# First layer: lower halves of the weights, keys, squares and mix halves move from GpSimd and VectorE

## The chip, the cores and the metric
The kernel runs on one core of one Trainium2 chip. The metric is device time in microseconds of one execution; a comparison uses medians of several. TensorE (PE) multiplies, VectorE (DVE) and ScalarE (ACT) work elementwise, GpSimd (POOL) works elementwise and issues DMAs, SyncE (SP) issues DMAs.

## The reference, cut to what matters
Two transformer-like blocks run one after the other. The change lies in the first layer of the first block, on 512 tokens and 256 tokens of context (768 columns):

```python
def even_mixer(hl, hc, w_in, lb, onorm_w, vnorm_w, ws, bs, w_out, with_ctx):
    pl = hl @ w_in                      # q, v, two z, g, u, v2
    ...
def hgrn2_features(p, lb):
    f = jnp.maximum(lb[d] + (1.0 - lb[d]) * jax.nn.sigmoid(z), F_MIN)
    log_f = jnp.log(f)
    k = 1.0 - f                         # the keys
# gla_chunked: per chunk, cumulated log_f, decays exp(b), scores, state update
def hgrn2_readout(o, g, onorm_w):
    o = rms_norm(o.transpose(0, 2, 1, 3), onorm_w).reshape(bsz, t_len, A_WIDTH)
    return (o * jax.nn.silu(g.astype(jnp.float32))).astype(g.dtype)
def chunk_mlp(u_pre, v_pre, vnorm_w, ws, bs):
    u = jax.nn.gelu(u_pre)
    v = rms_norm(jax.nn.gelu(v_pre)..., vnorm_w)
    sv = jnp.einsum('gts,bnsgc->bntgc', ws, v) + bs.T[:, :, None]
```

## The kernel before
Every operand of a large product is split into an upper half (rounded by ScalarE, `w_hi`) and a lower half (what is left, raw minus upper, `w_lo`); three matmuls make the product. `Flow` (from line 213) streams weight tiles of 128x1024: SyncE loads `w_raw` into two buffers, ScalarE makes `w_hi` at L337, VectorE makes `w_lo` at L393 or, where `low_on_pool` is set, GpSimd at L378, and TensorE multiplies (L456 in this stage). SyncE loads the next tile into a buffer once both halves of the old one are made. A flow has eight turns for each tile; an event is put at a turn, and `weave` merges several generators into one program for each engine by a list of nominal times. Each engine works its program off in order. Upper halves come at turn 1 (`split_turn`), one tile ahead of the products that use them.

`recurrence_and_mix` is the stage from 198 to 449 us. It weaves four things: the flow `uv` (8 tiles, gelu at L1450 by ScalarE), the flow `evg` (4 tiles, silu at L1583), the gated recurrence `Recurrence` (12 steps n over six chunks of 128 in two directions) and `ChunkMix` (4 groups). There are 13 lower halves in the stage: one at the start, one for each of the 12 tiles (two ahead).

A step n of the recurrence is spread over slots of 14.3 nominal us with eight turns. VectorE: `keys` (L1197, turn 3, three slots ahead), `sums` (scans, L1206, turn 7), `base_and_ends` (L1227, L1232), `levels` (L1216, L1217), `decayed_base` (L1244, L1245), `decayed` (L1255 to L1258), `merge` (L1277, L1280), `both` (L1288) and `update` of the state (L1298). ScalarE: `log` (L1310), `grow_base` and `grow` (L1318 to L1327), `keys_back` (L1332). TensorE: `read_out` (L1357, L1358), `gain` (L1365), transposes of the keys (L1374, waits for the update before), `scores` (L1385), `base_scores` (L1405). `keys(n)` waits for `mixed`, which `decayed(n-2)` gives, as both use the same buffer.

`ChunkMix`: ScalarE squares (L1474) and takes roots (L1480, L1485); VectorE norms (L1547); TensorE sums squares (L1510), transposes (L1524) and mixes (L1535); the gate product is L1460. `keep_busy` (L57) issues unread matmuls as fillers.

`GatedReadout` is the next stage, to 472.5 us. For four heads: squares of the output (L1640 by VectorE for heads 0 and 1, L1659 by GpSimd for 2 and 3), sums on TensorE (L1698), roots by ScalarE (L1680, L1683), norm (L1647) and gate product (L1653) by VectorE, upper half by ScalarE (L1673), lower half by VectorE (L1644). The four halves of the mix: upper by ScalarE (L1669), lower by GpSimd (L1662). TensorE ends with fillers once the last roots are made. The stage ends when all engines have ended. Then `eo` multiplies by `ev_out` (L474).

Of the kernel before, what the change touches and what calls it, by code (L numbers as in the profile page):

```python
# [4 lines left out]
F32 = mybir.dt.float32  # L5
F32R = mybir.dt.float32r
ALU = mybir.AluOpType
# [5 lines left out]
DT = D // P  # L13
# [201 lines left out]
class Flow:  # L215
# [10 lines left out]
    def __init__(self, K, c, name, w, n, kt, rhs_hi, rhs_lo, t0, T, on_act, on_dve, nxt, extra="", side=None,  # L226
                 rms_of=None, acc=None, after=None, split_turn=1, parts=1, then=1, ready=None, scaled=None,
                 makes=None, square=None, rms_ps=None, low_on_pool=False):
        nc = K.nc
# [5 lines left out]
        self.on_act, self.on_dve, self.split_turn, self.ready = on_act, on_dve, split_turn, ready  # L235
        self.given_acc, self.scaled, self.makes, self.low_on_pool = acc, scaled, makes, low_on_pool
        if acc is not None and acc[0].shape[1] == 1024:
            first = 512 - Scaled.PAIR - CTX
            self.acc = [a[:, first:first + Scaled.PAIR + T] if scaled is not None else a[:, 1024 - T:1024]
                        for a in acc]  # L240
        else:
            self.acc = [a[:, 0:T] if parts == 1 else a[:, :] for a in acc] if acc is not None else [
                c.enter_context(nc.psum_tensor(f"{name}_acc{j}", [P, 1024], F32))[:, 1024 - T:1024] for j in range(2)]
# [139 lines left out]
    def dve(self, dve):  # L383
# [30 lines left out]
        events = [(turn, lambda i, f=f: f(dve, self, i)) for turn, f in self.on_dve]  # L414
        events.append((self.split_turn, lambda i: split(i + 2)))
        if self.makes is not None:
# [685 lines left out]
class Recurrence:  # L1102
# [82 lines left out]
    def dve(self, dve):  # L1185
# [7 lines left out]

        def keys(n):
            if n >= 2:
                dve.wait_ge(self.mixed, n - 1)
            nc.vector.tensor_scalar(self.heads(self.k[n % 2]), self.of_z(n), -1.0, 1.0,  # L1197
                                    ALU.mult, ALU.add).then_inc(self.k_done, 1)

        def sums(n):  # L1200
# [90 lines left out]
        def update(n):  # L1291
# [4 lines left out]
            for h in range(H):  # L1296
# [4 lines left out]
            last.then_inc(self.updated, 1)  # L1301
        yield from self.turns({0: [(0, merge)], 1: [(1, decayed_base)], 2: [(1, decayed)], 3: [(3, keys)],
                               4: [(0, both), (0, update)], 5: [(2, base_and_ends)], 6: [(2, levels)], 7: [(3, sums)]})

    def act(self, act):
        nc, NL = self.nc, self.NL

        def log(n):
            act.wait_ge(self.k_done, n + 1)
            nc.scalar.activation(self.of_z(n), self.of_z(n), ACT.Ln).then_inc(self.logged, 1)  # L1310
# [242 lines left out]
def recurrence_and_mix(K, A, h_hi, h_lo, q, v, z, y_mlp, weights, x, g, nxt):  # L1553

    nc = K.nc
    with ExitStack() as c:
# [6 lines left out]
        def taken(name, n, work):  # L1563
# [9 lines left out]
                    [(1, cm.gelus)], [(2, cm.gate)],  # L1573
                    (A["ev_g"], DT), acc=acc, parts=2, low_on_pool=True)
        space = [(cm.mixed, 2 * B_GROUPS), (cm.normed, B_GROUPS), (cm.gated, B_GROUPS - 1), (cm.gated, B_GROUPS)]

        def gates(act, f, i):
            act.wait_ge(*space[i])
            for part in range(2):
# [5 lines left out]
        flow_g = Flow(K, c, "evg", A["ev_g"], A_HEADS, DT, h_hi, h_lo, 0, TOK, [(1, gates)], [], nxt, acc=acc, parts=2,  # L1585
                      after=flow, then=2, low_on_pool=True)
        tile = 196 / (2 * B_GROUPS + A_HEADS + 1)
# [8 lines left out]
        with K.block() as block:  # L1596
            @block.sync
            def _(sp):
                gl.sp(sp)
                cm.sp(sp)  # L1600
                weave([], flow.sp(sp))
                weave([], flow_g.sp(sp))

            @block.gpsimd
            def _(pool):
                flow.pool(pool)
                flow_g.pool(pool)

            @block.scalar
            def _(act):  # L1610
                weave(order, flow.act(act), flow_g.act(act), gl.act(act), cm.act(act, flow))

            @block.vector
            def _(dve):
                weave(order, flow.dve(dve), flow_g.dve(dve), gl.dve(dve), cm.dve(dve))

            @block.tensor
            def _(pe):
                weave(order, flow.pe(pe), flow_g.pe(pe), gl.pe(pe), cm.pe(pe))


class GatedReadout:


    def __init__(self, K, c, o, g, weights, y_mlp, hi, lo):
        nc = self.nc = K.nc
        self.K, self.o, self.g, self.weights, self.y_mlp, self.hi, self.lo = K, o, g, weights, y_mlp, hi, lo
        self.sq = c.enter_context(nc.sbuf_tensor("gr_sq", [P, A_HEADS, TOK], F32))
        self.roots = c.enter_context(nc.sbuf_tensor("gr_roots", [P, 2, TOK], F32))
        self.ps = [c.enter_context(nc.psum_tensor(f"gr_ps{j}", [P, 1024], F32)) for j in range(A_HEADS)]  # L1630
        (self.squared, self.squared_late, self.total, self.logged, self.rooted, self.normed, self.gated, self.hi_done,
         self.mlp_hi) = K.signals(
             "gr", "squared squared_late total logged rooted normed gated hi_done mlp_hi")

    SQUARED = 2

    def dve(self, dve):
        nc, H, o = self.nc, A_HEADS, self.o
        for h in range(self.SQUARED):
            nc.vector.tensor_tensor(self.sq[:, h, :], o[:, h, :], o[:, h, :], ALU.mult).then_inc(self.squared, 1)  # L1640

        def lower(h):
            dve.wait_ge(self.hi_done, h + 1)
            nc.vector.tensor_tensor(self.lo[h], o[:, h, :], self.hi[h].bitcast(F32), ALU.subtract)  # L1644
        for h in range(H):
            dve.wait_ge(self.rooted, h + 1)
            nc.vector.scalar_tensor_tensor(out=o[:, h, :], in0=o[:, h, :], scalar=self.weights[:, h:h + 1],  # L1647
                                           in1=self.roots[:, h % 2, :], op0=ALU.mult,
                                           op1=ALU.mult).then_inc(self.normed, 1)
            if h:  # L1650
                lower(h - 1)
            dve.wait_ge(self.normed, h + 1)
            nc.vector.tensor_tensor(o[:, h, :], o[:, h, :], self.g[h], ALU.mult).then_inc(self.gated, 1)  # L1653
        lower(H - 1)

    def pool(self, pool):
        nc, H, o = self.nc, A_HEADS, self.o
        for h in range(self.SQUARED, H):
            nc.gpsimd.tensor_tensor(self.sq[:, h, :], o[:, h, :], o[:, h, :], ALU.mult).then_inc(self.squared_late, 1)  # L1659
        for h in range(H):  # L1660
            pool.wait_ge(self.mlp_hi, h + 1)
            nc.gpsimd.tensor_tensor(self.lo[H + h], self.y_mlp[:, h, :], self.hi[H + h].bitcast(F32), ALU.subtract)  # L1662

# [26 lines left out]
    def pe(self, pe):  # L1690
        nc, H = self.nc, A_HEADS
        for h in range(H):
            if h < self.SQUARED:
                pe.wait_ge(self.squared, h + 1)
            else:
                pe.wait_ge(self.squared_late, h + 1 - self.SQUARED)
            for col, width in ((256, 256), (512, 512)):
# [7 lines left out]
def layer0(K, nc, A, x, x_back, col, cols, mods, mod0, scale1, y_hi, y_lo):  # L1705
# [6 lines left out]
    with ExitStack() as even_:  # L1712
# [4 lines left out]
        with ExitStack() as hctx:  # L1717
# [22 lines left out]
            with ExitStack() as c:  # L1740
                r = GatedReadout(K, c, q, g, col("onorm"), y_mlp, [y_hi[:, m, :] for m in range(DT)],
                                 [y_lo[:, m, :] for m in range(DT)])
                with K.block() as block:  # L1743
                    @block.sync
                    def _(sp):
                        sp.dma_start(x[:, 0:4, :], A["x"][:, 0:4, :]).then_inc(x_back, 16)
                        for h, k in enumerate(tiles):
                            sp.wait_ge(r.gated, h + 1)
                            sp.dma_start(x[:, k, :], A["x"][:, k, :]).then_inc(x_back, 16)

                    @block.gpsimd
                    def _(pool):
                        r.pool(pool)

# [2175 lines left out]
```

## Time and profile before
| | us |
|---|---|
| timed, median of 3 runs | 2685.71 (2684.73 to 2686.37) |
| the profiled execution | 2684.99 |
| its span | 2682.8 |
| mean granted clock of TensorE | 0.986 |
| PE, DVE, ACT, POOL busy | 2529.6, 1682.8, 988.9, 159.0 |

The rows of a timeline are: start in us, duration in us, engine, line, operation, output and inputs by the program's names, shapes, how many were merged into the row, and in brackets the idle time of the engine before it with what ended it. A row of the windows is: from:to, its length, busy us and count of PE, PEld (weight loads), DVE, ACT, POOL, then the granted clock of TensorE, the DMA share and GB/s. A row of the waits is: engine and what waited, who released it, us in total, times, longest. A row of the groups of instructions is: count, busy us, mean ns | idle time before and who ended it.

### The profile page before, as it was taken

The numbers are of one execution on the slowest core, as the hardware profiler recorded it, in microseconds if no ns is written. First come the engines' busy times: TensorE is split into PE (matmuls) and PEld (weight loads), VectorE is DVE, ScalarE is ACT, GpSimd is POOL, SyncE is SP. The second block draws the span as 40 slices with busy tenths as digits, with TensorE's granted clock in tenths as the row PEclk, the third lists the DMA queues.
The fourth block names the chain that finished last, engine by engine and source line by source line (L and its number), as shares of the span: only waits on it lengthen the run. The fifth ranks groups of instructions, "written<-read, shape, count | busy, mean of one in ns | idle before, by whom it ended". The sixth has DMA issues, their size and how long they took to land. (4 is left out here: it accounts for less than half of the span.)

```text
span 2682.8 us, 36507 instructions
## 1 busy us (share of the span) xinstructions
PE 2529.6 (94%) x14797; PEld 2135.6 (80%) x14797; DVE 1682.8 (63%) x2710; ACT 988.9 (37%) x1362; POOL 159.0 (6%) x167
## 2 busy tenths in 40 slices
PE   7999998999999999988999999999989988989997
PEld 2888887888888888865679989977778886867786
DVE  4887697467777776544446756746977774354744
ACT  4225565332212222344344322325542224344532
POOL 0110112000000000000000000000600000000000
PEclk9999999999999999999999999999999999999998
DMA  6650011323343333221013444322220000212232
GB/s 241 191 164 32 25 32 48 103 87 91 104 146 125 103 98 107 75 68 50 1 55 117 130 148 126 124 81 79 79 73 9 17 17 32 102 52 70 80 104 82
DMA packets 62680, 232.25 MB, mean 87 GB/s; under 512 B 6961, under 2 KB 9649, under 8 KB 61874
## 3 DMA queue, kind: packets, MB, share of 16 engines
q1 hardware_dynamic: 47538, 175.40, 20.1%
q0 software_dynamic: 14976, 54.53, 6.6%
q8 instruction: 117, 1.92, 0.3%
q14 instruction: 49, 0.40, 0.1%
HBM read 227.02 MB, written 2.10 MB: 85 GB/s over the span
## 5 line engine op out<-in xcount | busy, mean ns | idle before, releaser
L393 DVE TENSOR_TENSOR w_lo<-w_raw,w_hi 128x1024 fp32r<-128x1024 f32 (+4 forms) x271 | 334.5, 1234 | 375.0 <-ACT w_hi L337 370.8
L337 ACT ACTIVATE w_hi<-w_raw 128x1024 fp32r<-128x1024 f32 (+4 forms) x284 | 298.1, 1050 | 258.8 <-PE late_acc L474 93.4
L474 PE MATMUL mid_acc<-mid_h_hi,w_hi 128*128 128x258 f32 x832 | 279.4, 336 | 1.5 <-DVE mid_od_fq L642 1.0
L474 PE MATMUL mid_acc<-mid_h_hi,w_lo 128*128 128x258 f32 x832 | 279.0, 335 | 0.0
L474 PE MATMUL mid_acc<-mid_h_lo,w_hi 128*128 128x258 f32 x832 | 277.1, 333 | 0.0
L474 PE MATMUL late_acc<-late_h_hi,w_hi 128*128 128x258 f32 x704 | 199.3, 283 | 0.0
L474 PE MATMUL late_acc<-late_h_hi,w_lo 128*128 128x258 f32 x704 | 198.4, 282 | 0.0
L474 PE MATMUL late_acc<-late_h_lo,w_hi 128*128 128x258 f32 x704 | 197.7, 281 | 0.0
L474 PEld LDWEIGHTS mid_acc<-mid_h_hi,w_hi 128*128 128x128 f32 x832 | 157.3, 189 | 19.3 <-issue 2.4
L474 PEld LDWEIGHTS mid_acc<-mid_h_lo,w_hi 128*128 128x128 f32 x832 | 157.5, 189 | 18.6 <-issue 1.2
L474 PEld LDWEIGHTS mid_acc<-mid_h_hi,w_lo 128*128 128x128 f32 x832 | 156.8, 189 | 16.1
L474 PEld LDWEIGHTS late_acc<-late_h_lo,w_hi 128*128 128x128 f32 x704 | 133.6, 190 | 0.5 <-issue 0.5
L474 PEld LDWEIGHTS late_acc<-late_h_hi,w_hi 128*128 128x128 f32 x704 | 133.1, 189 | 0.5 <-issue 0.5
L474 PEld LDWEIGHTS late_acc<-late_h_hi,w_lo 128*128 128x128 f32 x704 | 132.7, 188 | 0.0
L474 PE MATMUL mid_acc<-mid_y_lo,w_hi 128*128 128x256 f32 (+1 forms) x384 | 128.7, 335 | 0.0
L474 PE MATMUL mid_acc<-mid_y_hi,w_hi 128*128 128x256 f32 (+1 forms) x384 | 128.3, 334 | 0.3 <-PEq L1743 0.3
L474 PE MATMUL mid_acc<-mid_y_hi,w_lo 128*128 128x256 f32 (+1 forms) x384 | 128.5, 335 | 0.0
L131 DVE CUSTOM_DVE_ANT_0 mid_scratch<-mid_side_raw,mid_rows 128x1024 f32<-128x1024 f32 x96 | 117.4, 1223 | 1.9 <-DVE mod L136 0.3
L2983 ACT ACTIVATE dr_low<-dr_bank 128x512 f32<-128x512 f32 x48 | 28.7, 597 | 174.5 <-PE dr_bank L3114 174.5
L474 PE MATMUL dq_acc<-s_h_hi,w_hi 128*128 128x512 f32 x200 | 85.3, 426 | 6.4 <-DVE s_h_lo L2569 5.1
L474 PE MATMUL qvz_acc<-ev_h_hi,w_hi 128*128 128x256 f32 (+1 forms) x256 | 87.2, 341 | 1.5 <-DVE ev_h_lo L936 1.5
L474 PE MATMUL qvz_acc<-ev_h_lo,w_hi 128*128 128x256 f32 (+1 forms) x256 | 86.9, 339 | 0.0
(531 smaller groups left out, 6176.8 us busy)
## 6 DMA issues: line engine op xcount, KB each, us to landing
w_raw<-in_up SPq DMA_DIRECT2D x88, 512.0 KB, 3.6
mid_side_raw<-in_ada_t POOLq DMA_DIRECT2D x48, 512.0 KB, 3.9
w_raw<-in_down SPq DMA_DIRECT2D x32, 704.0 KB, 4.0
qvz_side_raw<-in_ada_t POOLq DMA_DIRECT2D x32, 512.0 KB, 4.0
w_raw<-in_dn_qkv SPq DMA_DIRECT2D x25, 512.0 KB, 3.2
late_side_raw<-in_ada_t POOLq DMA_DIRECT2D x24, 512.0 KB, 4.0
w_raw<-in_da SPq DMA_DIRECT2D x18, 512.0 KB, 3.3
w_raw<-in_ev_qvz SPq DMA_DIRECT2D x16, 512.0 KB, 3.6
```

Of the source, the lines that this page charges most:

```text
L131: nc.vector.tensor_tensor_reduce(out=self.scratch, in0=self.raw[:, j, :], in1=self.rows[:, m, :], scale=1.0, scalar=0.0, op0=ALU.mult, op1 ...
L337: nc.scalar.activation(K.whi[:, g % 2, 0:width], K.raw[:, g % 2, 0:width], ACT.Copy).then_inc(K.hi_done, 1)
L393: nc.vector.tensor_tensor(K.wlo[:, g % 2, 0:width], K.raw[:, g % 2, 0:width], K.whi[:, g % 2, 0:width].bitcast(F32), ALU.subtract).then_in ...
L474: last = nc.tensor.matmul(self.acc[i % len(self.acc)][:, at:at + width], left[:, j, cols], right[k][:, moving:moving + width], start=(k == ...
L2983: nc.scalar.activation(XL[G][:, :], bank[G][0][:, :], ACT.Copy).then_inc(A[G].empty, 1)
```

## The change
Lower halves in the flows `uv` and `evg` are made by VectorE, at turn 5 of the tile (`low_turn=5`) instead of by GpSimd right after the upper half. The keys are made by ScalarE, right ahead of the logarithm of the same step, as an activation with scale -1 and bias 1. In the read-out all four squares and the four lower halves of the mix are VectorE's, each of the latter ahead of its head's norm. GpSimd has no part in either stage.

```diff
...
                  rms_of=None, acc=None, after=None, split_turn=1, parts=1, then=1, ready=None, scaled=None,
-                 makes=None, square=None, rms_ps=None, low_on_pool=False):
+                 makes=None, square=None, rms_ps=None, low_on_pool=False, low_turn=None):
...
         self.given_acc, self.scaled, self.makes, self.low_on_pool = acc, scaled, makes, low_on_pool
+        self.low_turn = split_turn if low_turn is None else low_turn
...
         events = [(turn, lambda i, f=f: f(dve, self, i)) for turn, f in self.on_dve]
-        events.append((self.split_turn, lambda i: split(i + 2)))
+        events.append((self.low_turn, lambda i: split(i + 2)))
...
-        def keys(n):
-            if n >= 2:
-                dve.wait_ge(self.mixed, n - 1)
-            nc.vector.tensor_scalar(self.heads(self.k[n % 2]), self.of_z(n), -1.0, 1.0,
-                                    ALU.mult, ALU.add).then_inc(self.k_done, 1)
...
             last.then_inc(self.updated, 1)
-        yield from self.turns({0: [(0, merge)], 1: [(1, decayed_base)], 2: [(1, decayed)], 3: [(3, keys)],
-                               4: [(0, both), (0, update)], 5: [(2, base_and_ends)], 6: [(2, levels)], 7: [(3, sums)]})
+        yield from self.turns({0: [(0, merge)], 1: [(1, decayed_base)], 2: [(1, decayed)], 4: [(0, both), (0, update)], 5: [(2, base_and_ends)], 6: [(2, levels)], 7: [(3, sums)]})
         def log(n):
+            if n >= 2:
+                act.wait_ge(self.mixed, n - 1)
+            nc.scalar.activation(self.heads(self.k[n % 2]), self.of_z(n), ACT.Identity, scale=-1.0,
+                                 bias=self.K.ones[:, 0:1]).then_inc(self.k_done, 1)
...
                     [(1, cm.gelus)], [(2, cm.gate)],
-                    (A["ev_g"], DT), acc=acc, parts=2, low_on_pool=True)
+                    (A["ev_g"], DT), acc=acc, parts=2, low_turn=5)
...
         flow_g = Flow(K, c, "evg", A["ev_g"], A_HEADS, DT, h_hi, h_lo, 0, TOK, [(1, gates)], [], nxt, acc=acc, parts=2,
-                      after=flow, then=2, low_on_pool=True)
+                      after=flow, then=2, low_turn=5)
...
-            @block.gpsimd
-            def _(pool):
-                flow.pool(pool)
-                flow_g.pool(pool)
...
         self.ps = [c.enter_context(nc.psum_tensor(f"gr_ps{j}", [P, 1024], F32)) for j in range(A_HEADS)]
-        (self.squared, self.squared_late, self.total, self.logged, self.rooted, self.normed, self.gated, self.hi_done,
+        (self.squared, self.total, self.logged, self.rooted, self.normed, self.gated, self.hi_done,
-             "gr", "squared squared_late total logged rooted normed gated hi_done mlp_hi")
-    SQUARED = 2
+             "gr", "squared total logged rooted normed gated hi_done mlp_hi")
         nc, H, o = self.nc, A_HEADS, self.o
-        for h in range(self.SQUARED):
+        for h in range(H):
         for h in range(H):
+            dve.wait_ge(self.mlp_hi, h + 1)
+            nc.vector.tensor_tensor(self.lo[H + h], self.y_mlp[:, h, :], self.hi[H + h].bitcast(F32), ALU.subtract)
...
         lower(H - 1)
-
-    def pool(self, pool):
-        nc, H, o = self.nc, A_HEADS, self.o
-        for h in range(self.SQUARED, H):
-            nc.gpsimd.tensor_tensor(self.sq[:, h, :], o[:, h, :], o[:, h, :], ALU.mult).then_inc(self.squared_late, 1)
-        for h in range(H):
-            pool.wait_ge(self.mlp_hi, h + 1)
-            nc.gpsimd.tensor_tensor(self.lo[H + h], self.y_mlp[:, h, :], self.hi[H + h].bitcast(F32), ALU.subtract)
...
         for h in range(H):
-            if h < self.SQUARED:
-                pe.wait_ge(self.squared, h + 1)
-            else:
-                pe.wait_ge(self.squared_late, h + 1 - self.SQUARED)
+            pe.wait_ge(self.squared, h + 1)
...
                             sp.dma_start(x[:, k, :], A["x"][:, k, :]).then_inc(x_back, 16)
-
-                    @block.gpsimd
-                    def _(pool):
-                        r.pool(pool)
                     def _(act):

```

## Rows read from the trace of the kernel before

**Rows 1.** Windows: busy time of each engine, recurrence stage and read-out.
```profile
198.00:449.30 251.30, 233.89 (x1596) 209.58 (x1596) 194.90 (x450) 140.30 (x186) 31.93 (x13) 0.97 0.09 29
449.30:472.50 23.20, 13.61 (x52) 10.16 (x52) 18.91 (x14) 14.33 (x17) 12.70 (x6) 0.71 0.44 134
```
**Rows 2.** Waits of TensorE, 196 to 474 us.
```profile
PE cm_ps L1524 <- DVE x L1547: 4.5, 2, 2.7
PE gl_bank L1374 <- DVE ev_rest L1298: 4.3, 4, 2.3
PE cm_ps L1510 <- ACT x L1474: 4.1, 1, 4.1
```
**Rows 3.** Groups of instructions: POOL over all; DVE by form; DVE and ACT, 196:450.
```profile
L378 POOL TENSOR_TENSOR w_lo<-w_raw,w_hi 128x1024 fp32r<-128x1024 f32 x13 | 31.9, 2457 | 225.3 <-ACT w_hi L337 225.3
...
L393 DVE TENSOR_TENSOR w_lo<-w_raw,w_hi 128x1024 fp32r<-128x1024 f32 x214 | 265.3, 1240 | 272.8 <-ACT w_hi L337 268.7 <-DMA dr_joins<-in_dr_joins 2.6
...
L1197 DVE TENSOR_SCALAR x<-ev_z 128x512 f32<-128x512 f32 x12 | 5.1, 425 | 1.1 <-DMA rstd<-in_gla_masks 0.8
...
L1310 ACT ACTIVATE ev_z<-ev_z 128x512 f32<-128x512 f32 x12 | 7.6, 629 | 13.6 <-DVE x L1197 13.6
```
**Rows 4.** Timeline around the third norm, DVE and then PE.
```profile
284.25 1.01 DVE L1547 SCALAR_TENSOR_TENSOR x<-x,cols 128x768 f32<-128x768 f32 x1
...
285.41 0.52 PE L1524 MATMUL cm_ps<-ident,x 128*128 128x128 f32 x3 [2.73 <-DVE x L1547]
```
**Rows 5.** Timeline of DVE ahead of the fifth update; the key is left out.
```profile
336.17 0.69 DVE L1258 TENSOR_TENSOR ev_z<-ev_q,ev_z 128x512 f32<-128x512 f32 x1
...
337.23 1.12 DVE L1298 SCALAR_TENSOR_TENSOR ev_rest<-ev_rest,gl_eb_end,gl_bank 128x128 f32<-128x128 f32 x4
```
**Rows 6.** Timeline of DVE in eight places of the recurrence stage.
```profile
204.00 0.40 DVE L1197 TENSOR_SCALAR x<-ev_z 128x512 f32<-128x512 f32 x1
...
249.84 3.48 DVE L1206 TENSOR_TENSOR_SCAN ev_z<-ones,ev_z 128x128 f32<-128x128 f32 x4
...
259.96 1.02 DVE L1547 SCALAR_TENSOR_TENSOR x<-x,cols 128x768 f32<-128x768 f32 x1 [0.84 <-ACT x L1485]
...
353.21 1.12 DVE L1298 SCALAR_TENSOR_TENSOR ev_rest<-ev_rest,gl_eb_end,gl_bank 128x128 f32<-128x128 f32 x4 [0.39 <-PE gl_bank L1365]
...
387.03 1.12 DVE L1298 SCALAR_TENSOR_TENSOR ev_rest<-ev_rest,gl_eb_end,gl_bank 128x128 f32<-128x128 f32 x4 [0.17 <-PE gl_bank L1365]
...
403.25 1.12 DVE L1298 SCALAR_TENSOR_TENSOR ev_rest<-ev_rest,gl_eb_end,gl_bank 128x128 f32<-128x128 f32 x4
...
412.33 2.12 DVE L1244 TENSOR_TENSOR ev_rest<-x,ev_rest 128x512 f32<-128x512 f32 x1
...
447.88 1.12 DVE L1298 SCALAR_TENSOR_TENSOR ev_rest<-ev_rest,gl_eb_end,gl_bank 128x128 f32<-128x128 f32 x4 [0.21 <-PE gl_bank L1365]
```
**Rows 7.** Timeline of the read-out: POOL, DVE and the fillers of PE.
```profile
455.89 2.13 POOL L1662 TENSOR_TENSOR mid_y_lo<-ev_y_mlp,mid_y_hi 128x768 fp32r<-128x768 f32 x1 [0.36 <-ACT mid_y_hi L1669]
...
456.38 2.46 DVE L1653 TENSOR_TENSOR ev_q<-ev_q,x 128x768 f32<-128x768 f32 x1
...
461.24 0.94 DVE L1644 TENSOR_TENSOR mid_y_lo<-ev_q,mid_y_hi 128x768 fp32r<-128x768 f32 x1
...
465.65 6.63 PE L57 MATMUL gr_ps<-ident 128*128 128x128 f32 x36 [8.32 <-ACT gr_roots L1683]
...
470.92 0.96 DVE L1644 TENSOR_TENSOR mid_y_lo<-ev_q,mid_y_hi 128x768 fp32r<-128x768 f32 x1 [0.91 <-ACT mid_y_hi L1673]
```
**Rows 8.** Timeline of ACT: the exponential of step 10.
```profile
411.83 2.33 ACT L1327 ACTIVATE ev_rest<-ev_rest 128x2560 f32<-128x2560 f32 x1
```
**Rows 9.** Windows: the 4 us after TensorE's idle time, three places.
```profile
285.40:289.40 4.00, 3.99 (x23) 4.00 (x24) 2.88 (x9) 1.46 (x2) 0.00 (x0) 0.61 0.00 0
...
311.20:315.20 4.00, 4.00 (x34) 3.88 (x35) 2.83 (x9) 1.52 (x2) 0.00 (x0) 1.00 0.02 4
...
338.40:342.40 4.00, 4.00 (x30) 3.74 (x30) 4.00 (x11) 3.26 (x5) 0.00 (x0) 1.00 0.01 2
```

## The prediction
> **What bounds the kernel now.** I read the busy time by stage first [rows 1]. The change touches two stages. In the recurrence stage (198.0 to 449.3 us) TensorE is busy 233.9 of 251.3 us, VectorE 194.9, ScalarE 140.3, GpSimd 31.9: TensorE is the bound, and only what lengthens or shortens its 17 us of idle time moves the stage's end. In the read-out (449.3 to 472.5) VectorE is busy 18.9 of 23.2 us and TensorE is idle for half. Next the waits of TensorE [rows 2]: in the recurrence it waits 4.5 us for the norm of the chunk mix (L1547, twice), 4.3 us for the state update (L1298, four times), 4.1 us for a square on ScalarE (L1474). The first two are VectorE's, in a queue that runs in program order; so the question for each lower half put into that queue is whether it stands ahead of L1547 or L1298 at a moment when TensorE already waits. Last the timelines around those waits [rows 4 to 6]. The later slots run at 16 us each with both TensorE and VectorE nearly full.
>
> **Costs of one instruction** [rows 3]. A lower half of 1024 columns takes 1.24 us on VectorE; back-to-back instructions start 0.09 us before the one ahead ends (the norm of 1.01 us at 284.25 [rows 4] follows such a pair), so it moves what stands behind it by 1.15 us. On GpSimd it took 2.46 us, and nobody waited for it. A key on VectorE took 0.43 us and moved the next start by 0.46 (336.17 + 0.69 - 0.09 = 336.77 against 337.23, [rows 5]). On ScalarE it is an activation of the logarithm's shape, 0.63 us, so the logarithm comes about 0.24 us later in each of 12 steps. Its next work in the slot is the copy of the transposed keys, which waits for TensorE, and it idles 251.3 - 140.3 = 111 us in the stage: I take nothing, at most 12 x 0.24 = 2.9 us if that cover is gone. No lower half should be waited for directly: turn 5 of 8 leaves three turns, 3/8 of a 16 us slot or 6 us less VectorE's lag, before its tile starts on TensorE; and the reload of the raw weights, which SyncE issues after the lower half, has a whole tile of time. Both at nothing; what they cost without that cover is rival (c).
>
> **The port.** GpSimd slows VectorE now. Beside a GpSimd instruction from 455.89 to 458.02, the gate product that takes 0.95 us took 2.46 [rows 7]: it ended 0.8 us after GpSimd did. In the recurrence six VectorE instructions are held that way, four by 2.1 us (as in [rows 6] at 249.84: four scans in 3.48 us instead of 1.37), one by 1.45 (412.33) and one by 0.4, together 10.4 us; the others beside GpSimd read PSUM and aren't held. The Trainium skill (SBUF — State Buffer, Who interferes with whom) says that a VectorE instruction with two SBUF inputs and a GpSimd one that reads SBUF block each other whole, the second waiting for the first; by this rule, the trace agrees. Most of these 10.4 us fall where VectorE waits for TensorE right afterwards, so they aren't on the path; the one at 412.33 is.
>
> **Recurrence stage, lower half by lower half.** In the order of the woven program the 13 lower halves land as follows.
> 1. First (before the scans of step 0): VectorE waits for ScalarE there anyway, and one key less (204.00 [rows 6]) brings the base decays forward 0.3 us. ScalarE's chain hangs on that up to the square at L1474: -0.3.
> 2. Tile 0, ahead of the first norm: TensorE runs fillers there: 0.
> 3. Tile 1, ahead of the second norm: VectorE idled 0.84 us before it (259.96 [rows 6]); 1.15 less that idle and the overlap of 0.08 leaves +0.2.
> 4. Tiles 2 and 3, each right ahead of the third and fourth norm, for which TensorE waits (285.41 [rows 4]): +1.15 each, +2.3. The block at 249.84 doesn't help: it lies long before.
> 5. Tile 4, between the decays and the update at 337.23, for which TensorE waits 2.3 us [rows 2, 5]: 336.77 + 1.15 = 337.92, +0.7.
> 6. Tiles 5, 6, 7: the update idled 0.39, 0.39, 0.17 us for TensorE before it (353.21 and 387.03 are the first and last of the three, [rows 6]); 1.15 - 0.46 - idle - 0.09 (the overlap that an idle costs) gives +0.2, +0.2, +0.4.
> 7. First tile of the gate weights, ahead of the sum and update at 403.25, no idle: +0.7.
> 8. In the next slot the held instruction at 412.33 (2.12 us) is freed of 1.45, of which 0.7 counts, since the decays then wait for the exponential that ends at 414.16 [rows 8]; the wait of TensorE for the update there was 0.7: -0.7.
> 9. Next two lower halves lie after the update, ahead of merges that wait for TensorE's scores: 0 (1.15 each, 2.3, if those waits are gone).
> 10. The last stands behind the last update (447.88 + 1.12 = 449.00 [rows 6]) and is then the stage's last instruction, where GpSimd's ran beside the update: +1.15.
> Sum: -0.3 + 0.2 + 2.3 + 0.7 + 0.8 + 0.7 - 0.7 + 1.15 = **+4.9 us**. Bounds: +1.15 alone if TensorE catches up in every slot, +7.8 if the ScalarE cover is gone too.
>
> **Read-out.** VectorE gets 2 squares and 4 lower halves more (0.94 us long [rows 7], 0.87 from start to start) and loses the blocks, 6.1 us in five instructions. Walked, with ScalarE's order kept: four squares from 449.3 to 452.9, first lower half of the mix to 453.8, then roots at 455.1 as before; from there per head a mix lower, a norm, a lower half and a gate, 3.7 us, with hardly a wait. The last roots are ready at 463.8 instead of 465.6, VectorE ends at 469.8 instead of 471.9. The stage ends with TensorE's fillers (6.63 us from 465.65 to 472.28 [rows 7]), which start with the last roots: 470.5, so **-1.8 us**. Bounds: 0, if the squares delay the second head's roots, and -2.1.
>
> **The clock.** After TensorE's idle 2.7 us up to 285.41 its granted clock was 0.61 in the next 4 us, the low of the two levels (1.2 and 2.4 GHz) for most of it, and 23 matmuls ran; after 1.7 us idle up to 311.17 it stayed at 1.00, and 34 ran [rows 9]. The missing 11 of 34 are 1.3 us. After 2.3 us up to 338.40 it held 1.00 too. With the change these two idles become 2.9 and 3.0 us, longer than the one that was followed by the fall. I take one fall, **+1.3**; 0 and 2.6 are the ends. [...]
>
> **Sum.** +4.9 - 1.8 + 1.3 = +4.4 us. The profiled execution took 2684.99 (span 2682.8), the three timed ones 2684.73 to 2686.37, median 2685.71; the sum is made on its rows and goes onto the median: 2690.1.
>
> **Rivals.**
> (a) *VectorE's total decides, not its places.* Added 13 x 1.15 = 15.0, gone 12 x 0.43 = 5.1 and 10.4 of blocks: -0.5, with the read-out -2.3: 2683.4. For it: VectorE is nearly full from 340 to 425. Against it: TensorE is as full there, and the blocks lie before VectorE's waits. To be faster by over 5.4 us it would need gains that no row shows.
> (b) *The waits lengthen and the clock falls with them* (slower). Place: the norms and the update of item 4 and 5; it decides once TensorE's idles there pass the 2.7 us of the row with a fall. Two falls give +5.7, 2691.4; a third, from the idle at 285.41 which grows to 3.9 us, +7.0, 2692.7.
> (c) *The lower half comes too late* for the tile or the reload, since VectorE may lag by more than the 6 us: the later tiles, 8 by 1 us each on top of the sum, 2698.
> (d) *The keys' activation forces a reload of function tables* on ScalarE. The program uses the same function beside logarithm and exponential elsewhere (L875), so I give it next to nothing; it is in (c).
>
> **How the numbers follow.** A measurement tells about 0.2% from no change, 5.4 us: 2680.3 to 2691.1. Forecast 0.42 (own range 2687 to 2691, a little of it over the line), (a) 0.22, (b) 0.28, (c) with (d) 0.08. Faster: a third of (a), 0.08. Slower: most of (b), (c) and a seventh of the forecast, 0.36. Same: 0.56. The range takes (a) and (b) in with their bounds: 2682.5 to 2694.
>
> **What would show it.** TensorE's waits for L1547 grow from 4.5 to about 6.8 us, those for the update by about 1.5; the last instruction of the recurrence stage is a lower half on VectorE, some 5 us later than 449.0 (6 with the fall); no VectorE instruction is over 1.3 us in the read-out, which lasts 21.4 instead of 23.2. Low clock appears in one new place between 309 and 345. It is wrong if the stage's end moves by less than 2 us, if ScalarE becomes what TensorE waits for, or if new waits for lower halves appear.

## The result and the profile after

The changed kernel took 2695.6 us, median of 7 runs (2692.34 to 2697.53), against 2686.01 of the kernel before, median of 7 runs on the same chip (2682.84 to 2688.57): ratio 1.0034, 95% interval 1.0025 to 1.0043. It is slower by 9.6 us; the forecast was 2690.1, its range ended at 2694.0. The profiled execution has a span of 2693.5 us, 10.7 more than before. The ratios below leave out two odd executions on one chip, 6683.4 us of before_fill and 5084.06 us of the kernel before.

First the windows of the kernel after, over the recurrence and the read-out, in the columns of [rows 1]; as there, the second starts with VectorE's first square of the read-out:
```profile
199.20:465.00 265.80, 241.79 (x1596) 216.90 (x1596) 194.41 (x451) 148.97 (x198) 0.00 (x0) 0.94 0.08 27
465.00:485.60 20.60, 12.60 (x52) 9.25 (x52) 18.06 (x20) 14.09 (x17) 0.00 (x0) 0.75 0.46 143
```
The recurrence stage takes 265.8 us and not 251.3, the read-out 20.6 and not 23.2.
TensorE executes the same 1596 matmuls, yet is busy 241.8 us and not 233.9, at a mean granted clock of 0.94 and not 0.97. VectorE's busy time is no more than before (194.4 against 194.9). The total on VectorE decides nothing here; idle places and the clock do.

The waits of TensorE from 197 to 486 us, kernel after, against [rows 2]:
```profile
PE cm_ps L1522 <- DVE x L1545: 6.7, 2, 3.9
PE gr_ps L57 <- ACT gr_roots L1668: 6.6, 1, 6.6
PE cm_ps L1508 <- ACT x L1472: 6.4, 3, 5.5
PE gl_bank L1372 <- DVE ev_rest L1293: 5.2, 4, 3.0
```
The norm (L1545, before L1547) is waited for 2.2 us longer, the update (L1293, before L1298) 0.9 longer, and the square (L1472, before L1474) three times instead of once.

The first of the long waits in the timeline of VectorE and then of TensorE, kernel after, to be laid beside [rows 4]:
```profile
287.26 1.22 DVE L394 TENSOR_TENSOR w_lo<-w_raw,w_hi 128x1024 fp32r<-128x1024 f32 x1
288.39 1.01 DVE L1545 SCALAR_TENSOR_TENSOR x<-x,cols 128x768 f32<-128x768 f32 x1
...
289.55 0.87 PE L1522 MATMUL cm_ps<-ident,x 128*128 128x128 f32 x3 [3.87 <-DVE x L1545]
...
317.31 0.55 PE L1522 MATMUL cm_ps<-ident,x 128*128 128x128 f32 x3 [2.88 <-DVE x L1545]
...
346.82 1.11 PE L1372 MATMUL gl_bank<-ident,ev_rest 128*128 128x128 f32 x4 [3.01 <-DVE ev_rest L1293]
```
A lower half stands right ahead of the norm that TensorE waits for. The three idles are 3.87, 2.88 and 3.01 us; the forecast had 3.9, 2.9 and 3.0. The same three transposes take 0.87 us behind the first idle and 0.55 behind the second; at full clock before they took 0.52 [rows 4].

The clock around these idles: a window of the kernel after that takes in 2 us on either side of the end of the first idle, then four from just ahead of the end of the third (346.82):
```profile
287.50:291.50 4.00, 1.95 (x10) 1.98 (x10) 3.88 (x8) 2.48 (x2) 0.00 (x0) 0.56 0.42 119
...
346.20:350.20 4.00, 3.38 (x17) 3.38 (x17) 4.00 (x12) 2.20 (x3) 0.00 (x0) 0.50 0.42 133
350.20:354.20 4.00, 4.00 (x14) 3.42 (x14) 3.38 (x9) 3.97 (x7) 0.00 (x0) 0.50 0.00 0
354.20:358.20 4.00, 4.00 (x18) 3.81 (x18) 0.88 (x2) 2.92 (x3) 0.00 (x0) 0.50 0.00 0
358.20:362.20 4.00, 4.00 (x19) 3.32 (x19) 1.42 (x3) 0.00 (x0) 0.00 (x0) 0.81 0.00 0
```
From 346.0 to 359.7 us, 13.7 us, TensorE is at the lower of its two levels (0.50 of full clock), although from the end of the third idle on, 12.9 us of it, it is busy without a gap. Before, the 4 us at this place held 30 matmuls at clock 1.00 [rows 9]; here it is 14 to 18.

**The ledger.** Both kernels issue the same 14797 matmuls in the same order, so each can be laid beside its counterpart and the shift (start after, less start before) read along the stage. In us, beside the forecast:

| place (time before) | shift grows by | forecast |
|---|---|---|
| stage start to first square (198.2 to 216.5) | +0.1 | -0.3 |
| second square on ScalarE (251.4) | +0.86 | 0 |
| second norm (261.0) | +0.2 | +0.2 |
| third square on ScalarE (274.3) | +0.64 | 0 |
| third and fourth norm (285.4, 311.2) | +1.18, +1.10 | +2.3 |
| fifth update (338.4) | +0.85 | +0.7 |
| the next three updates | +0.4 | +0.8 |
| gate weights (404.4) | +0.67 | +0.7 |
| freed decays (420.6) | -0.78 | -0.7 |
| last lower half (450.3) | +1.14 | +1.15 |
| places together | +6.3 | +4.9 |
| behind the idle at 285 | +0.9 | |
| behind the idle at 311 | +1.45 | |
| behind the idle at 338 | +5.8 | |
| clock together | +8.2 | +1.3 |
| read-out (22.2 to 19.7 us) | -2.5 | -1.8 |

A row takes in what crept in since the row above: at the second square the step at the wait itself is 0.62, and the other 0.24 came mostly at 221.5 us, where TensorE was at the upper level again before and still at the lower after; at the fifth update the step is 0.69. The last rows on the clock are differences from the first trace of before, which has a fall of its own at 286 us. So recurrence and read-out are 12.0 us longer together. The stage starts 1.2 us later in this execution and the rest of the program takes 2.4 us less: that is the span's 10.7.

### The profile page after: what moved, and what is told of

It reads as the page before. It is cut to its first block and busy times, and to the rows that moved or that the text cites. A ratio compares the mean times of both kernels' runs of the same rounds, so it can differ in the third digit from the quotient of the medians.

```text
span 2693.5 us, 36505 instructions
## 1 busy us (share of the span) xinstructions
PE 2536.0 (94%) x14797; PEld 2142.4 (80%) x14797; DVE 1680.7 (62%) x2717; ACT 997.4 (37%) x1374; POOL 113.4 (4%) x148
## 5 line engine op out<-in xcount | busy, mean ns | idle before, releaser
L394 DVE TENSOR_TENSOR w_lo<-w_raw,w_hi 128x1024 fp32r<-128x1024 f32 (+4 forms) x284 | 350.2, 1233 | 374.4 <-ACT w_hi L338 368.9
```

Source lines behind the costliest of these rows:

```text
L394: nc.vector.tensor_tensor(K.wlo[:, g % 2, 0:width], K.raw[:, g % 2, 0:width], K.whi[:, g % 2, 0:width].bitcast(F32), ALU.subtract).then_in ...
```

## The experiments

Each edit is against the kernel named. "Low clock" adds up the stretches at the lower level that begin after 221 us and end before the first sum of the read-out, by the trace's own record of the granted clock; "recurrence" is from the first matmul of its flow to the first of the read-out's sums. One profiled execution each. A filler of the program shows as two matmuls in the rows (15 fillers as x30):

| kernel | idles ahead of 3rd norm, 4th norm, 5th update | low clock, us | recurrence, us |
|---|---|---|---|
| before, three executions | 2.73, 1.74, 2.31 | 3.4, 3.4, 10.2 | 252.2, 252.7, 256.2 |
| after, three executions | 3.87, 2.88, 3.01 | 23.9, 17.0, 23.9 | 266.7, 264.1, 266.7 |
| low_only | 3.87, 2.88, 3.34 | 13.6 | 263.2 |
| three_early | 3.87, 2.88, 3.01 | 17.0 | 263.1 |
| turn7 | 2.73, 1.74, 1.88 | 6.8 | 255.6 |
| fill | 0.42, 0.42, 0.33 | 0 | 256.4 |
| before_fill | 0.40, 0.40, 0.55 | 3.4 | 252.8 |
| turn7_fill | under 0.6 | 0 | 252.7 |
| turn7_more | under 0.6 | 0 | 248.6 |
| readout_only | 2.73, 1.74, 2.32 | 10.2 | 256.3 |
| keys_only | 2.73, 1.74, 1.85 | 10.2 | 255.1 |
| before_start | 2.73, 1.74, 2.31 | 10.2 | 253.0 |

### Which part does it: the read-out alone, the lower halves alone, the keys alone

**readout_only.** The kernel before with the new read-out; GpSimd still makes the lower halves.
```diff
-        for h in range(self.SQUARED):
+        for h in range(H):
...
+            dve.wait_ge(self.mlp_hi, h + 1)
+            nc.vector.tensor_tensor(self.lo[H + h], self.y_mlp[:, h, :], self.hi[H + h].bitcast(F32), ALU.subtract)
```


> The kernel before with the new read-out alone (squares and the mix's lower halves on VectorE). Theory (blocks on the shared port go, in the whole change the read-out was 2.5 us shorter): the stage of 23.2 us becomes 20.5 to 21.5, the total 1.8 to 2.6 us less than before, ratio 0.9990 to 0.9993. Rival (VectorE has 6 instructions more and is the bound there, so the stage grows by part of 5.2 us): 2 us more.


Measured: 2683.95 us against 2686.23, ratio 0.9991 (0.9982 to 0.9999). From its first sum to the first matmul of the next stage the read-out took 19.7 instead of 22.2 us. This part of the change gains 2.5 us in the stage and it isn't eaten elsewhere. In the trace of the kernel after, VectorE's part of the read-out begins:
```profile
465.01 3.56 DVE L1631 TENSOR_TENSOR gr_sq<-ev_q 128x768 f32<-128x768 f32 x4 [0.32 <-PEq L1594]
468.49 0.95 DVE L1638 TENSOR_TENSOR mid_y_lo<-ev_y_mlp,mid_y_hi 128x768 fp32r<-128x768 f32 x1
470.79 1.02 DVE L1640 SCALAR_TENSOR_TENSOR ev_q<-ev_q,cols,gr_roots 128x768 f32<-128x768 f32 x1 [1.36 <-ACT gr_roots L1668]
471.85 0.96 DVE L1646 TENSOR_TENSOR ev_q<-ev_q,x 128x768 f32<-128x768 f32 x1
...
479.47 5.75 PE L57 MATMUL gr_ps<-ident 128*128 128x128 f32 x36 [6.60 <-ACT gr_roots L1668]
```
The gate product takes 0.96 us where it took 2.46 beside GpSimd [rows 7].

**low_only.** The kernel after with keys on VectorE and the read-out of before, so that only the 13 lower halves are moved.
```diff
+        def keys(n):
+            if n >= 2:
+                dve.wait_ge(self.mixed, n - 1)
+            nc.vector.tensor_scalar(self.heads(self.k[n % 2]), self.of_z(n), -1.0, 1.0,
+                                    ALU.mult, ALU.add).then_inc(self.k_done, 1)
```


> The kernel before with the 13 lower halves on VectorE at turn 5 alone; keys and read-out stay. Theory (delays ahead of norms and updates, and TensorE's clock falls behind the longer idles): the recurrence stage is longer by 13 to 16 us, as in the whole change (14.4), since each update now also has the key ahead of it (+0.46 each), less ScalarE's 1.7; total +12 to +16 us. Rival (the keys on ScalarE made most of the loss): below +6 us.


Measured: 2695.59 us, ratio 1.0033 (1.002 to 1.0045), recurrence 263.2, 11.0 more than before, where 13 to 16 were expected: this execution had 13.6 us of low clock, the first of after 23.9. TensorE's gaps of 0.45 us at the second and third square are absent, its idles at the norms are those of the kernel after. The lower halves alone make a loss as large as the whole change, which has the read-out's gain in it.

**keys_only.** The kernel before with the keys on ScalarE, as in the change's `log`, and nothing else.
```diff
...
         def log(n):
+            if n >= 2:
+                act.wait_ge(self.mixed, n - 1)
+            nc.scalar.activation(self.heads(self.k[n % 2]), self.of_z(n), ACT.Identity, scale=-1.0,
+                                 bias=self.K.ones[:, 0:1]).then_inc(self.k_done, 1)
```


> The kernel before with the keys of the recurrence on ScalarE and nothing else; lower halves stay on GpSimd. Theory (ScalarE's cover was thin at the squares it makes): TensorE waits 0.4 to 0.5 us at the second and third square of ScalarE, each about 0.85 us later than before, +1.7; VectorE is 0.46 us earlier at the fifth update and some of those behind it, -0.5 to -1.8. Together 0 to +1.2 on the recurrence of 252.2. Forecast's view (the keys are covered on ScalarE): recurrence 250.5 to 252, no gap of TensorE behind a square of ScalarE.


Measured: 2685.57 us against 2686.24, ratio 0.9993 (0.9984 to 1.0002): no change that can be told. The ledger against before shows -0.94 at the first square, +0.62 at the second and at the third and -0.47 at the fifth update, which nearly cancel; behind the idles there and at 377 us the shift grows from 0.38 to 3.28 in low clock. The timeline of TensorE in keys_only has the gap in question:
```profile
251.47 0.91 PE L1507 MATMUL cm_ps<-x,ones 128*128 128x384 f32 x2 [0.46 <-ACT x L1471]
```
The groups of instructions of ScalarE in the kernel after, 196 to 464 us (count, busy us, mean ns), show the two activations:
```profile
L1305 ACT ACTIVATE x<-ev_z,ones 128x512 f32<-128x512 f32 x12 | 8.6, 719 | 7.9 <-DVE ev_z L1253 7.9
L1308 ACT ACTIVATE ev_z<-ev_z 128x512 f32<-128x512 f32 x12 | 7.6, 632 | 0.4
```
The key takes 0.72 us, 0.09 more than the logarithm of the same shape; its bias is read from a tile. And ScalarE's queue is not covered at these two squares, which come 0.62 us later each, as in the kernel after.

### Are the idles the cause of the low clock: fillers, and later turns

**fill.** The kernel after with fillers ahead of the three waits, so that TensorE doesn't idle; nothing starts earlier.
```diff
-                    K.keep_busy(self.ps[:, 0:P], (12, 6, 0, 4)[g])
+                    K.keep_busy(self.ps[:, 0:P], (12, 6, 15, 15)[g])
...
+            if n == 5:
+                self.K.keep_busy(self.ps_s[0][:, 0:P], 12)
```


> The changed kernel with unread fillers on TensorE in the three longer idles: 15 in place of 0 and 4 ahead of the third and fourth norm (3.9 and 2.9 us of idle), 12 ahead of the wait for the fifth update (3.0 us). Theory (8 of the 14.4 us are TensorE at the low clock behind those idles: 6.8, 3.4 and 13.7 us at 0.5 against 3.4 before): the low stretches between 285 and 360 us go, total 7 to 10 us below the changed kernel, 2686 to 2689. Rival (the pace after those idles is VectorE's or ScalarE's, and the low clock costs nothing): within 1.5 us of the changed kernel, 2694 to 2697.


Measured: 2685.71 us, ratio 0.9997 (0.9987 to 1.0006), recurrence 256.4, which is 10.3 less than after. The windows of fill at the places of the three falls:
```profile
286.00:317.00 31.00, 30.16 (x219) 26.72 (x219) 22.30 (x50) 17.19 (x23) 0.00 (x0) 1.00 0.12 35
317.00:345.00 28.00, 27.43 (x195) 24.34 (x195) 21.67 (x53) 16.47 (x24) 0.00 (x0) 1.00 0.07 20
345.00:379.00 34.00, 32.83 (x243) 30.54 (x241) 32.68 (x76) 21.82 (x27) 0.00 (x0) 1.00 0.10 31
```
and the same of the kernel after:
```profile
286.00:317.00 31.00, 24.88 (x150) 21.65 (x150) 19.93 (x42) 17.74 (x25) 0.00 (x0) 0.89 0.06 17
317.00:345.00 28.00, 26.26 (x174) 23.41 (x174) 20.04 (x49) 13.39 (x20) 0.00 (x0) 0.94 0.07 20
345.00:379.00 34.00, 32.18 (x183) 29.55 (x184) 27.27 (x65) 21.11 (x27) 0.00 (x0) 0.80 0.09 32
```
No work was taken away and nothing that TensorE waits for was put earlier in a queue; unread matmuls were added, and 9.9 us of run time went. This shows that the idles led to the low clock and that the low clock is the larger part of the loss. The remaining recurrence agrees with the ledger: 252.2 of before, less 1.6 for its own fall, plus the places' 6.3, is 256.9, and 256.4 was measured.

**turn7.** The kernel after with the lower halves at turn 7 in both flows, behind the norms and the update.
```diff
-                    (A["ev_g"], DT), acc=acc, parts=2, low_turn=5)
+                    (A["ev_g"], DT), acc=acc, parts=2, low_turn=7)
...
```


> The changed kernel with the lower halves at turn 7 in place of 5: in program order they then stand behind the norms and behind the updates. Theory (the place ahead of norm and update makes the delays, and these the longer idles): the idles at norms and update are again 2.7, 1.7 and 2.3 us, no long low clock, the recurrence stage is 1 to 3 us longer than before (ScalarE's squares 1.7 and the last lower half 1.15, less 0.8 of the freed block), total 2684 to 2688. Rival (VectorE's total, not the place, or the lower half now too late for its tile): 2693 or more, with waits of TensorE for lower halves.


Measured: 2685.70 us, ratio 0.9997 (0.9988 to 1.0005), recurrence 255.6. The idles are back at 2.73 and 1.74, the update's at 1.88, since the key is gone from VectorE. Here it is the waits themselves that are shortened, with the same gain as from the fillers.

**three_early.** turn7, with the lower halves of tiles 2, 3 and 4 of the first flow back at turn 5: these stand ahead of the third norm, the fourth norm and the fifth update.
```diff
-        events.append((self.low_turn, lambda i: split(i + 2)))
+        early = (2, 3, 4) if self.name == "uv" else ()
+        events.append((self.low_turn, lambda i: split(i + 2) if i not in early else None))
+        events.append((5, lambda i: split(i + 2) if i in early else None))
```


> The changed kernel with the lower halves at turn 7, but three of the 13 (tiles 2, 3 and 4, ahead of the third and fourth norm and the fifth update) left at turn 5. Theory (these three places make the longer idles, 3.9, 2.9 and 3.0 us, and all of the low clock): nearly all of the loss comes back, 3.2 us of idle and 4 to 8 of clock on top of turn 7's 2685.7, so 2692 to 2696. Rival (the delay is spread over all 13 places): 3/13 of the difference of 10 us, 2687 to 2689.


Measured: 2693.07 us, ratio 1.0029 (1.0019 to 1.0039), recurrence 263.1. Three of 13 lower halves, moved by two turns, cost 7.4 us by the medians (on two chips) and 7.5 by the recurrence; the ratios are 0.9997 and 1.0029. On the path they add 3 x 1.15 = 3.4 us at most; the rest is the low clock, 17.0 us of it against 6.8.

**before_fill** and **turn7_fill.** Fillers ahead of the same three waits, in the kernel before (8 at the update) and in turn7 (7).
```diff
-                    K.keep_busy(self.ps[:, 0:P], (12, 6, 0, 4)[g])
+                    K.keep_busy(self.ps[:, 0:P], (12, 6, 10, 10)[g])
...
```


> The kernel before with fillers in the same three idles: 10 in place of 0 and 4 ahead of the third and fourth norm (2.7 and 1.7 us of idle), 8 ahead of the wait for the fifth update (2.3 us). Theory (an idle of that size is followed by the low clock in some executions and not in others: the profile of before had one stretch of 3.4 us, that of the kernel with the new read-out alone 10.2 us behind the unchanged update): 1 to 4 us below before, and no low clock between 230 and 440 us. Rival (the low clock there costs nothing, or the fillers delay the work behind them): within 0.5 us or more than before.

> Lower halves at turn 7 and fillers in the three idles that are left (10, 10 and, ahead of the fifth update, 7). Theory: both gains add, the low stretches of 3.4 us at 289 and 343 go: 1.5 to 3.5 us below turn 7 alone, 2682 to 2684. Rival: turn 7 had already taken all that the clock cost, within 1 us of 2685.7.


Measured: before_fill 2684.56 us (median of the other ten), ratio 0.9998 (0.9988 to 1.0007), a miss: the fall at 286 us is gone, but one of the same 3.4 us stands at 377, behind an idle of 1.75 us that got no fillers, and the recurrence is 252.8. turn7_fill 2682.18 us, ratio 0.9984 (0.9975 to 0.9993), no low clock between 224 and 452 us, recurrence 252.7. So the same fillers were worth nothing that can be told in before, 0.0013 of the ratio in turn7 and 10 us in after, which has the most low clock of the three.

### Is one trace of the clock enough

> The kernel before itself, a second look at its clock. Its first trace has one low stretch between 221 and 449 us, 3.4 us long, behind the idle of 2.73; three variants of it (only the read-out, only the keys, only fillers at the start) have two or three, 10.2 us together, behind idles of 2.3 and 1.75. Theory (the idles of before lead to low clock in some executions, and the first trace was a good one): 3 to 10 us of low clock in that stretch, recurrence 252 to 256. Rival (the kernel before falls once, always): 3.4 us behind 286, recurrence 252.0 to 252.4.

> The kernel before once more, for the same question: theory 3 to 10 us of low clock and recurrence 252 to 256, rival 3.4 us and 252.0 to 252.4.

> The changed kernel itself, a second look: does the low clock last as long in another execution? In the first trace it lasted 6.8, 3.4 and 13.7 us behind idles of 3.87, 2.88 and 3.01 us, 23.9 together. Theory (the idles lead to it, its length varies): the idles are the same within 0.05, low clock behind at least two of the three, 14 to 27 us together. Rival (one odd execution was caught): one fall or none, under 10 us together, and a span 5 us shorter than 2693.5.

> The changed kernel, a third look. Two traces had 23.9 and 17.0 us of low clock between 221 us and the read-out, recurrence 266.7 and 264.1. Theory (idles of 3 us and more fall in nearly every execution, the length varies): 13 to 24 us, recurrence 262 to 267. Rival (both were bad executions): under 10 us, recurrence under 261.


Measured: before 3.4 us of low clock and 252.7, then 10.2 us and 256.2; after 17.0 us and 264.1, then 23.9 us and 266.7. The whole executions took 2684.99, 2686.04 and 2685.63 us before and 2695.6, 2693.34 and 2699.07 after; the one of before with 10.2 us of low clock in this stage isn't longer, as the low clock of the whole program is 77.9, 76.8 and 76.7 us in the three, and the 3.5 us by which the third of after exceeds the first lie behind this stage. The idles are the same to within 0.01 us in all three executions of each kernel; the clock isn't. Windows from 338 us, before_again (idle ends 340.27) and before_third (337.94):
```profile
342.00:346.00 4.00, 4.00 (x30) 3.70 (x30) 4.00 (x12) 3.96 (x5) 0.00 (x0) 1.00 0.00 0
346.00:350.00 4.00, 4.00 (x23) 3.44 (x22) 3.73 (x8) 3.91 (x6) 2.41 (x1) 1.00 0.19 19
```
```profile
338.00:342.00 4.00, 4.00 (x23) 3.81 (x24) 4.00 (x11) 3.33 (x5) 0.00 (x0) 0.66 0.00 0
342.00:346.00 4.00, 4.00 (x17) 3.61 (x16) 2.70 (x7) 3.90 (x7) 2.15 (x1) 0.50 0.00 0
346.00:350.00 4.00, 4.00 (x16) 3.45 (x16) 0.88 (x2) 1.86 (x1) 0.22 (x1) 0.56 0.39 131
```
The same program, the same idle of 2.3 us: no fall in one execution and 10.2 us of low clock in the other. The rival for before (always one fall) fell, and so did mine that 3.4 us was merely lucky: it came twice in three. Averages over three: 5.7 us before, 21.6 after.

Nor is every idle followed by a fall. Counted over all traces here, with a fall that begins between 1.6 us ahead of an idle's end and 2.1 behind it:

| idle, us | where | followed by low clock |
|---|---|---|
| 3.87 | third norm | 5 of 5 |
| 3.0 to 3.34 | fifth update | 5 of 5 |
| 2.88 | fourth norm | 2 of 5 |
| 2.73 | third norm | 5 of 7 |
| 2.31 | fifth update | 3 of 5 |
| 1.85, 1.88 | fifth update | 2 of 2 |
| 1.75 | 375 to 392 us | 5 of 16 |
| 1.74 | fourth norm | 0 of 7 |

In after_again the idle of 2.88 us had no fall behind it; its three falls stand at the third norm, at the fifth update and at 388 us.

### How far can it be taken

**turn7_more.** turn7_fill with four edits more: 20 fillers ahead of the first square, 4 at the end of the recurrence, 4 at the start of the read-out, and the last lower half earlier, so that it isn't the stage's last instruction.
```diff
...
+        events.append((3, lambda i: split(i + 2) if last and i == self.n - 1 else None))
...
+            if n == self.n - 1:
+                self.K.keep_busy(self.ps_s[0][:, 0:P], 4)
...
+                    if g == 0:
+                        K.keep_busy(self.ps[:, 0:P], 20)
...
+        self.K.keep_busy(self.ps[3][:, 0:P], 4)
...
```


> The one before, with three more steps: 20 fillers in the idle of 5.5 us ahead of the first square, 4 at the end of the recurrence and 4 at the start of the read-out, and the last lower half at turn 3, ahead of the last sum instead of behind the last update. Theory: the last lower half no longer ends the stage, -1.0; the low clock behind 217 us goes, and with it up to 2 us, as the fillers and transposes there are TensorE's own work; the sums of the read-out run at the high level, -1: 2 to 4 us below the one before, 2679 to 2681. Rival (after 217 the merges wait for VectorE and ScalarE, whatever the clock): only the last lower half's 1.0.


Measured: 2676.06 us, median of 5 runs (2674.09 to 2679.24), ratio 0.9966 (0.9953 to 0.9979): faster than both kernels, by 9 us against before and 19 against after, and 3 us faster than was expected at best. Recurrence 248.6, read-out 18.3. Two of its windows; from 221 to 446 us the clock is 1.00 throughout:
```profile
221.00:286.00 65.00, 63.95 (x456) 56.35 (x455) 38.13 (x86) 34.78 (x52) 0.00 (x0) 1.00 0.06 17
...
345.00:379.00 34.00, 31.75 (x232) 29.49 (x231) 33.32 (x78) 22.18 (x29) 0.00 (x0) 1.00 0.17 47
```

**before_start.** The kernel before with the 20 fillers alone.
```diff
+                    if g == 0:
+                        K.keep_busy(self.ps[:, 0:P], 20)
```


> The kernel before with one edit: 20 fillers of TensorE ahead of its wait for the first square of the chunk mix. In the kernel before TensorE idles 5.5 us there and its granted clock is low for 6.8 us from 214.6. In the fastest kernel so far four things were changed at once, and the recurrence fell from 252.7 to 247.6 us. Theory (the clock at the start of the stage is what that gain came from): no low clock from 214.6, recurrence 252.2 less about 4 = 248, median about 2682. Rival (the gain came from the place of the last lower half, 1.1, and of the other fillers): recurrence 251 to 252, median 2685 to 2686.


Measured: 2684.02 us against 2686.24, ratio 0.9992 (0.9983 to 1.0001), so not told apart from no change, and the recurrence of the profiled execution is 253.0, not 248. The low clock at the start, 6.8 us from 214.6 before, is gone, as expected; but two falls of 3.4 us came at 339.5 and 377.1, behind the idles of 2.31 and 1.75 us that were always there. The 247.6 us of the expectation run to the read-out's first filler; to its first sum, as everywhere else here, it is 248.6. The clock at the start is not shown to be turn7_more's gain. How the 4.1 us of recurrence that it has over turn7_fill divide among its four edits was not tried one by one; the last lower half is worth 1.14 by the ledger.

## Why the prediction was wrong

**Right.** What bounds the stage, and where a lower half is on the path. The three idles came as forecast (3.87, 2.88, 3.01), the wait for the norm as 6.7 for 6.8, second norm as 0.2 for 0.2, third and fourth norm as 2.28 for 2.3, fifth update 0.85 for 0.7, gate weights 0.67 for 0.7, freed decays -0.78 for -0.7, last lower half 1.14 for 1.15. Those terms come from the rule "the lower half costs 1.15 where it stands ahead of an instruction that TensorE waits for, nothing where VectorE idles before it". The stage's last instruction is a lower half, as forecast, but it ends 15.7 us later than the last update of before (464.7 against 449.0), not 5 or 6. No new wait for a lower half appeared, and ScalarE has no more loads of function tables than before, 26 against 27 in the stage's groups; (c) and (d) fell. Rival (a), that VectorE's total decides, fell with the three idles.

**Wrong, the clock term.** The step that failed is "I take one fall, +1.3; 0 and 2.6 are the ends". Its price for one fall of 3.4 us was nearly right, 1.3 us: against before_third, which has no fall there, the one at 286 us cost before 1.6. In before_third 10.2 us cost 4.8 (its shift against before grows from -0.5 to +4.3), and behind the third idle of the kernel after 13.7 us cost 5.8, which is 0.47, 0.47 and 0.42 for each microsecond. What was wrong is how many falls there are and how long each lasts: in the first trace all three idles were followed by one, and lengths were 6.8, 3.4 and 13.7 us where I had one of 3.4 besides the one of before. One row was taken as the length of every fall, and one that showed clock 1.00 behind 2.3 us of idle [rows 9] as evidence that 2.3 us is safe. before_third shows that it isn't. Against the first trace of before the term was 8.2, 5.6 and 8.2 us in three executions of after, and 5.8 between the means of three and three, where the forecast had 1.3 and at most 2.6.

Rival (b) had the mechanism, waits that lengthen and a clock that falls with them, and even the third place; it gave 2692.7 because it too counted 3.4 us a fall. The Trainium skill (TensorE: Matmul & The Clock Gate, What's actually happening) says of a kernel's start that the number of matmuls at the low rate varies from run to run of one and the same kernel, and that the ramp costs under 1% of a typical span. Nothing here looks at a kernel's start; of falls in its middle the traces show the same: 3.4 to 10.2 us before, 17.0 to 23.9 after, and a price of 8 in 2686 us, 0.3%. That is small for a kernel and, with the 6.3 us of the places, what decided this change.

**Wrong, the cover on ScalarE.** "I take nothing" for the keys' activation: two squares came late, 0.62 and 0.64 us at the waits and +1.5 with what crept in ahead of them, where the forecast's bound was 2.9. The idle sum of 111 us said nothing about these two places; keys_only shows the same two gaps without any lower half moved.

**Small misses.** The three middle updates cost 0.4 for 0.8, the start +0.1 for -0.3. That +0.1 hides two larger parts: counted from the stage's first matmul, the first square came 1.4 us later in low_only and 1.0 earlier in keys_only than in the first trace of before; the three traces of before lie within 0.3. So the first lower half did stand on that path, where item 1 of the prediction put nothing for it, and the key's leaving paid for it. The read-out gained 2.5 for 1.8: 1.86 up to the fillers, as forecast, and the rest because the 36 fillers took 5.75 us instead of 6.63 [rows 7] at a higher clock; the walk had left them at their old length.

**The sum.** Between the means of three traces the recurrence is 12.1 us longer (265.8 against 253.7), places 6.3 and clock 5.8, and the read-out 2.3 shorter (20.1 against 22.4), together +9.9 us; the medians differ by 9.6.

**Open.** What sets how long a fall lasts: 3.4 us and 13.7 us follow idles of 2.88 and 3.01 us, with TensorE busy in both. And why an idle of 1.75 us that every kernel here has was followed by a fall in 5 traces of 16.

## To carry to other kernels

Work moved onto an engine is priced by what stands behind it in that engine's queue, place by place; here that gave the three waits for VectorE to within 0.1 us. Then allow, beside each idle of TensorE that the change lengthens, for a stretch of low clock that can be several times longer than the idle, at 0.4 to 0.5 us a microsecond, and read it from more than one trace: one trace's clock is one draw. Put such work behind the instruction that TensorE waits for, not ahead of it (turn 7 and not 5 was worth 10 us here), and try fillers in the idles that remain (turn7_fill: 2682.2 for 2685.7 us).

## What was not expected of the hardware

- TensorE, busy 3.98 to 4.00 of each 4 us, stayed at the lower clock for 12.9 us from the end of an idle of 3.0 us on.
- The low clock can begin before the idle has ended: at 288.0 us, 1.5 us before TensorE had work again at 289.55.
- An idle of 1.75 us (at 377 to 388 us) was followed by 3.4 us of low clock in before_start, keys_only, before_fill, three_early and after_again, and by none in the three executions of before.
- before_start lost 6.8 us of low clock at 215 us and had two stretches of 3.4 us later that the first trace of before does not have. Whether the one brought the others isn't shown: keys_only has two such stretches with the fall at 215 us in place.
